# Softmax weights normalised before the transpose instead of attention outputs after the value product

## The reference, cut to what matters

```python
s = einsum(q, k) * scale;  s = where(valid, s, MASK_VALUE)
p = exp(s - max(s));  denom = sum(p);  num = einsum(p, v)
...
den = sum(wts[i] * branches[i][2] for i in range(len(branches)))
return (num / den[..., None]).astype(q.dtype)
```

## Time and profile before

| | us |
|---|---|
| median of 3 runs | 2556.98 (2556.7 to 2559.38) |
| profiled execution, first to last instruction | 2554.3 |
| TensorE busy | 2518.2 (99% of the span) |
| VectorE busy | 1324.1 (52%) |
| ScalarE busy | 567.3 (22%) |
| GpSimd busy | 1519.9 (60%) |

### The profile page before, as it was taken

One profiled execution on the slowest core, in us unless ns is written; L12 is line 12 of the kernel. 1 busy time (PEld: TensorE's weight loads), 2 busy tenths in 40 slices (PEclk: granted clock), 3 DMA queues, 4 the chain that ended last, 5 costly groups with the idle time before them and its releaser, 6 DMA issues.

```text
span 2554.3 us, 33028 instructions
## 1 busy us (share of the span) xinstructions
PE 2518.2 (99%) x11986; PEld 2058.2 (81%) x11986; DVE 1324.1 (52%) x1556; ACT 567.3 (22%) x1033; POOL 1519.9 (60%) x858
## 2 busy tenths in 40 slices
PE   8999999999999999999999999999999988999998
PEld 6888888778888888888888778888887766888887
DVE  6555527656555315556137656555227656655512
ACT  2110014652111001110015552011013564111000
POOL 5666666436666666666665536666664322666664
PEclk9999999999999999999999999999999999999999
DMA  5233222113223223222322113232323111322232
GB/s 169 94 99 99 94 96 75 59 42 98 92 98 99 97 93 99 98 92 98 99 92 74 51 49 99 97 116 98 99 98 134 50 42 34 99 97 93 98 99 74
DMA packets 66724, 228.67 MB, mean 90 GB/s; under 512 B 8784, under 2 KB 11728, under 8 KB 66256
## 3 DMA queue, kind: packets, MB, share of 16 engines
q1 hardware_dynamic: 64928, 225.67, 27.0%
q10 hardware_dynamic: 1712, 1.82, 0.2%
HBM read 225.36 MB, written 2.10 MB: 89 GB/s over the span
## 4 chain that ended last, share of the span: by engine, by line
PE 96%; DVE 2%; ACT 1%; issue 0%; POOL 0%; DMA 0%; SPq 0%; DVEq 0%; POOLq 0%; ACTq 0%
PE bank L610 28%; PE bank L611 28%; PE bank L612 28%; PE bank L627 2%; PE bank L769 2%; PE bank L754 2%; PE bank L738 1%; PE bank L633 1%; PE bank L739 1%; PE bank L992 1%; PE bank L1007 1%; PE bank L984 0%; PE bank L618 0%; PE bank L983 0%; PE bank L899 0%
## 5 line engine op out<-in xcount | busy, mean ns | idle before, releaser
L574 POOL TENSOR_TENSOR wl<-raw,wh 128x1024 fp32r<-128x1024 f32 x412 | 1037.1, 2517 | 34.4
L571 POOL TENSOR_SCALAR wh<-raw 128x1024 fp32r<-128x1024 f32 x412 | 444.8, 1080 | 981.9 <-PE bank L612 944.5
L610 PE MATMUL bank<-xh,wh 128*128 128x512 f32 x2096 | 818.6, 391 | 0.0
L611 PE MATMUL bank<-xl,wh 128*128 128x512 f32 x2096 | 816.4, 389 | 0.0
L612 PE MATMUL bank<-xh,wl 128*128 128x512 f32 x2096 | 816.3, 389 | 0.0
L612 PEld LDWEIGHTS bank<-xh,wl 128*128 128x128 f32 x2096 | 393.5, 188 | 82.7
L610 PEld LDWEIGHTS bank<-xh,wh 128*128 128x128 f32 x2096 | 393.5, 188 | 81.2 <-issue 0.2
L611 PEld LDWEIGHTS bank<-xl,wh 128*128 128x128 f32 x2096 | 393.6, 188 | 81.0 <-issue 0.2
L610 PE MATMUL bank<-acth,wh 128*128 128x512 f32 (+1 forms) x902 | 346.4, 384 | 0.0
L611 PE MATMUL bank<-actl,wh 128*128 128x512 f32 (+1 forms) x902 | 346.2, 384 | 0.0
L612 PE MATMUL bank<-acth,wl 128*128 128x512 f32 (+1 forms) x902 | 346.2, 384 | 0.0
(11 more groups left out here) (273 smaller groups left out, 2352.3 us busy)
## 6 DMA issues: line engine op xcount, KB each, us to landing
raw<-in_stream SPq DMA_DIRECT2D x412, 512.0 KB, 3.6
x<-in_x SPq DMA_DIRECT2D x8, 256.0 KB, 5.9
w1k<-in_w1k SPq DMA_DIRECT2D x1, 2048.0 KB, 9.0
w1v_low<-in_w1v SPq DMA_DIRECT2D x1, 1024.0 KB, 6.7
w1v_high<-in_w1v SPq DMA_DIRECT2D x1, 1024.0 KB, 8.9
out_dram<-x SPq DMA_DIRECT2D x4, 256.0 KB, 2.6
out_dram<-x SPq DMA_DIRECT2D x1, 768.0 KB, 3.7
invcount<-in_c_invcount ACTq DMA_DIRECT2D x1, 512.0 KB, 5.9
```

Source lines behind the costliest of these rows:

```text
L571: nc.gpsimd.tensor_scalar(wh[:, h, :, :], src, 1.0, 1.0, ALU.mult, ALU.mult)\
L574: nc.gpsimd.tensor_tensor(wl[:, h, :, :], src, wh[:, h, :, :].bitcast(F32), ALU.subtract).then_inc(split_done, 1)
L610: mm = nc.tensor.matmul(bank, wh[:, slot, k, :], rh, start=start, stop=False)
L611: mm = nc.tensor.matmul(bank, wh[:, slot, k, :], rl, start=False, stop=False)
```

## The change

Each step's weights are divided by their sum before the turn. VectorE gets `scale_weights(g)`: a reciprocal of one column of `sden`, a wait for it, and a `tensor_scalar` that multiplies the 128 x 512 weights in `sc` in place. It stands right behind the mask instruction of step g + 1. TensorE's `turn(g)` waits for it (`p_done`) and no longer for the exponential. The spread of the reciprocals, their transposes, the copy of the numerators and the product with the rows are gone, with their buffers `on` and `recb`. `high_output` and `low_output` read bank 7 itself, in steps 3 and 4 of the next pair; `values` of a pair waits until `low_output` of the pair before has read the bank. Waits on counts of `ml_done` and `mh_done` are renumbered to the new order.

```diff
@@ TensorE
                 def turn(g):
-                    pe.wait_ge(exp_done, l * STEPS + (g + 1))
+                    pe.wait_ge(p_done, l * STEPS + (g + 1))
...
-                def reciprocal_rows(j):
-
-                    pe.wait_ge(rb_done, l * PAIRS + (j + 1))
-                    pe.wait_ge(vtok_done, l * PAIRS + min(j + 2, PAIRS))
-                    for i in range(NQ):
-                        tr = nc.tensor.transpose(B[6][:, i * P:(i + 1) * P],
-                                                 recb[:, 2 * i:2 * i + 2, :].rearrange("p h d -> p (h d)"), ident[:, :])
-                    tr.then_inc(ot_done, 1)
@@ values
-                        pe.wait_ge(num_done, l * PAIRS + (j + 1))
+                        if l or j:
+                            pe.wait_ge(out_read, l * PAIRS + j)
@@ ScalarE
-                def spread_reciprocals(j):
-                    act.wait_ge(rec_done, l * PAIRS + (j + 1))
-                    nc.scalar.activation(recb[:, :, :], srec[:, :].rearrange("p (c a) -> p c a", a=1)
-                                         .to_broadcast([P, 8, HD]), ACT.Copy).then_inc(rb_done, 1)
-
-                def numerators(j):
+                def high_output(j):
                     act.wait_ge(pv_done, l * HALVES + (2 * j + 4))
-                    nc.scalar.activation(on[:, :], B[7][:, :], ACT.Copy).then_inc(num_done, 1)
-
-                def high_output(j):
-                    act.wait_ge(on_done, l * PAIRS + (j + 3))
-                    nc.scalar.activation(mh1[:, 2 + j, :], on[:, :], ACT.Copy).then_inc(mh_done, 1)
+                    nc.scalar.activation(mh1[:, 2 + j, :], B[7][:, :], ACT.Copy).then_inc(mh_done, 1)
@@ VectorE
-                def reciprocals(j):
-                    dve.wait_ge(exp_done, l * STEPS + (8 * j + 8))
-                    V.reciprocal(srec[:, :], sden[:, j % 2, :]).then_inc(rec_done, 1)
-
-                def normalise(j):
-                    dve.wait_ge(num_done, l * PAIRS + (j + 2))
-                    dve.wait_ge(ot_done, l * PAIRS + (j + 1))
-                    V.tensor_tensor(on[:, :], on[:, :], B[6][:, :], ALU.mult).then_inc(on_done, 1)
+                def scale_weights(g):
+                    e, s = g // 8 % 2, g % 8
+                    dve.wait_ge(exp_done, l * STEPS + (g + 1))
+                    V.reciprocal(srec[:, s:s + 1], sden[:, e, s:s + 1]).then_inc(rec_done, 1)
+                    dve.wait_ge(rec_done, l * STEPS + (g + 1))
+                    V.tensor_scalar(sc[:, g % 3, :], sc[:, g % 3, :], srec[:, s:s + 1], None, ALU.mult).then_inc(p_done, 1)
 
                 def low_output(j, done):
                     dve.wait_ge(mh_done, l * 8 + done)
-                    V.tensor_tensor(ml1[:, 2 + j, :], on[:, :], mh1[:, 2 + j, :].bitcast(F32), ALU.subtract)\
-                        .then_inc(ml_done, 1)
+                    V.tensor_tensor(ml1[:, 2 + j, :], B[7][:, :], mh1[:, 2 + j, :].bitcast(F32), ALU.subtract)\
+                        .then_inc(out_read, 1)
+                    dve.wait_ge(out_read, l * PAIRS + (j + 1))
+                    dve.nop().then_inc(ml_done, 1)
@@ VectorE's loop, step s of pair j
                         V.tensor_tensor_reduce(sc[:, g % 3, :], B[(5, 2)[g % 2]][:, :], band[:, off:off + T], 1.0,
                                                3.0e38, ALU.add, ALU.min, smin[:, s:s + 1]).then_inc(t_done, 1)
+                        if g:
+                            scale_weights(g - 1)
...
-                        if s == 1 and j > 0:
-                            reciprocals(j - 1)
                         if s == 4 and j > 0:
-                            normalise(j - 1)
+                            low_output(j - 1, j if more else 6)
...
-                        if s == 7 and j > 0:
-                            low_output(j - 1, j if more else 7)
```

More of the change, by code:

```diff
@@ L208, in build @@
         pt = sb("pt", [P, 4, T], at=mix1)
-        recb = sb("recb", [P, 8, HD], at=mix1)
         ropet = sb("ropet", [P, 2, T], at=mix1)
@@ L383, in build @@
         rec_done = sem("rec_done")
-        rb_done = sem("rb_done")
-        num_done = sem("num_done")
-        on_done = sem("on_done")
+        p_done = sem("p_done")
+        out_read = sem("out_read")
         zeroed = sem("zeroed")
-        ot_done = sem("ot_done")
         tr_done = sem("tr_done")
@@ L744, in value_turn @@
                     pe.wait_ge(v_evac, l * PAIRS + (j + 1))
-                    pe.wait_ge(on_done, l * PAIRS + (j + 1))
+                    if l or j:
+                        pe.wait_ge(vtok_done, l * PAIRS + j)
                     for kt in range(NQ):
@@ L797, in out_blocks @@
                             if m == 1:
-                                pe.wait_ge(ml_done, l * 8 + 7)
-                        pe.wait_ge(ml_done, l * 8 + (k if 1 < k < 6 else {0: 6, 1: 7, 6: 8, 7: 9}[k]))
+                                pe.wait_ge(ml_done, l * 8 + 8)
+                        pe.wait_ge(ml_done, l * 8 + (k if 1 < k < 6 else {0: 6, 6: 7, 1: 8, 7: 9}[k]))
                         mm = split_product(B[m][:, :], m % 2, k, mh1[:, k, :], ml1[:, k, :], start, stop)
@@ L822, in mixer1 @@
                             values(2 * j - 1)
-                        if s == 3 and j > 0:
-                            reciprocal_rows(j - 1)
                         if s == 6:
@@ L1280, in mixer1 @@
                         if s == 3 and j > 0:
-                            numerators(j - 1)
+                            high_output(j - 1)
                         if s == 4 and more:
                             high_q(l * PAIRS + (j + 1), 1 - e)
-                        if s == (5 if more else 6) and j > 0:
-                            high_output(j - 1)
                         if s == 6 and more:
@@ L1294, in mixer1 @@
                 copy_turn(STEPS - 1)
-                spread_reciprocals(PAIRS - 1)
-                numerators(PAIRS - 1)
                 high_output(PAIRS - 1)
@@ L1735, in pool_low @@
                 def pool_low(t):
[L1736 removed]
+                    dve.wait_ge(mh_done, l * 8 + (5, 7)[t])
                     V.scalar_tensor_tensor(ml1[:, t, :], B[1][:, :], poolscale[:, l, t:t + 1],
                                            mh1[:, t, :].bitcast(F32), ALU.mult, ALU.subtract).then_inc(ml_done, 1)
[L1740 to L1747 removed]
+                def scale_weights(g):
[4 more added lines that the diff above has]
+                    V.tensor_scalar(sc[:, g % 3, :], sc[:, g % 3, :], srec[:, s:s + 1], None, ALU.mult).then_inc(p_done, 1)
                 def low_output(j, done):
                     dve.wait_ge(mh_done, l * 8 + done)
[L1751 to L1752 removed]
+                    V.tensor_tensor(ml1[:, 2 + j, :], B[7][:, :], mh1[:, 2 + j, :].bitcast(F32), ALU.subtract)\
+                        .then_inc(out_read, 1)
+                    dve.wait_ge(out_read, l * PAIRS + (j + 1))
+                    dve.nop().then_inc(ml_done, 1)
                 for j in range(PAIRS):
@@ L1785, in mixer1 @@
                             pool_low(s // 6)
-                        if s == 7 and j > 0:
-                            low_output(j - 1, j if more else 7)
-                reciprocals(PAIRS - 1)
-                normalise(PAIRS - 1)
+                scale_weights(STEPS - 1)
                 low_output(PAIRS - 1, 8)
```

5 lines of the change are left out of this document (removed).

## The result

The kernel after takes 2614.05 us (median of 4 runs, 2610.87 to 2615.26), the kernel before beside it 2556.84: a ratio of 1.0218, 95% interval 1.0206 to 1.023. It is slower, as forecast, by 57 us instead of 39, and outside the range. The profiled execution took 2610.87 us with a span of 2608.7, 54.4 more than the span before; its mean clock was 0.994, that of the other three runs 0.992 to 0.994.

What follows compares the result with a forecast made beforehand. TensorE was taken as the bound, 96% of the chain that ended last. Per layer 22.15 us of new waits less 2.6 saved gave 19.5, 39 over two layers, added to 2557: 2596 us, range 2567 to 2612.

Steps and rivals of the forecast that it cites:

- What bounds the kernel: Whole kernel: TensorE is 96% of the chain that ended last; VectorE has room on average, but in steps with four fill blocks.
- the saving: TensorE: six groups of four transposes of `recb` per layer go, 0.44 us each, 5.3 us over two layers.
- The scaling's price: VectorE: reciprocal 0.15, own wait 0.02, multiplication 0.49, together 0.66 us; on meeting GpSimd it ends 0.28 behind GpSimd's instruction.
- The waits per pair: TensorE in pairs with fill: 2.0 us at step 4's turn, 0.85 at step 6's, 0.3 ahead of scores; 3.15 in all.
- the pooling: End of pairs 0 to 2: GpSimd's pooling step can hold the last low part of k; 1.5 us for the three.
- the sum: Loops of pairs: 22.15 us of new waits less 2.6 saved per layer, 39 us slower over two layers.
- The clock falls: Loops of pairs: waits of 2 us bring TensorE to half clock for a quarter of both loops, 80 us more; chance 0.02.
- VectorE finds the time: Loops of pairs: scalings fall into VectorE's idle stretches only, so the saving alone stays, 2551.7 us; chance 0.05.
- it changes nothing: Whole kernel: saving and waits cancel, 2557 us; chance 0.03.
- No meeting: VectorE's scalings do not wait for GpSimd; step 4's turn waits 0.75 us, total 2567 to 2568 us; chance 0.10.
- Half of it: Loops of pairs: GpSimd's instructions move with TensorE, some scalings miss them; some 25 us more, 2580 us; chance 0.10.

Runs made afterwards that it cites:

- The run with the reciprocals alone: Kernel after the change without the scalings' multiplication; the reciprocal and the turn's wait on it stay: 2555.62 us, ratio 0.9995.
- the run without the wait: Kernel after the change with scalings written to a spare buffer and the turn waiting only for the exponential: 2624.05 us, ratio 1.0265.

## Why the prediction was wrong, and what of it was right

**What bounds the kernel, and the saving**: right. TensorE's chain, idle time of VectorE in the wrong places, and 5.3 us of transposes gone. The run with the reciprocals alone gains only 1.2 of these (3.8 at most by its interval): some 1.7 us of waits stay in its two loops, and eight stops at 0.22 are 1.8 more.

**The scaling's price**: right. 0.16 and 0.49 us plain, and 0.28 behind GpSimd's instruction when it meets one. By the Trainium skill (VectorE: DVE Perf Modes, "The TRN2 errata") I had estimated 0.33 for the 0.49; the trace does not agree, the median of the 96 is 0.487.

**The waits per pair**: right in sum, and part by part only for pairs 1 to 3 and 5. Forecast were 3.15 for every pair with fill and 0.5 more for the pooling in pairs 0 to 2; measured in layer 0 are 3.5, 3.73 and 2.76 in pairs 1 to 3. Pair 4 had 1.70, and 2.65 at its end, where I had 3.15 and 2.3. Pair 5 had 2.6, as forecast. Pair 0 had 5.24, and 0.28 at its end, instead of 3.65; 4.63 of it is a wait that my working did not follow, the fill's on `rope`. That these errors cancel, to 0.1 us in layer 0 and 0.3 in layer 1, is luck.

**The step that failed** is the sum: "Per layer 15.75 + 1.5 + 2.3 + 2.6 = 22.15 us of new waits, less 2.6 saved". It prices a wait at its idle time and lets TensorE go on at its old pace. Two terms were missing, each taken as nothing. Some 41 stops (21 in the loop of layer 0, 20 in that of layer 1, six of them under 0.1 us) at 0.22 are 9.0 us. Stretches at half clock of 3.41, 3.41 and 6.83 us are 13.65 us; 2.28 of these lie in a stop, and in the other 11.4 a matmul begins 0.43 us after the one before it where it was 0.23, so some 5.3 us are lost. With both the sum is 22.2 + 21.9 - 5.3 + 9.0 + 5.3 = 53.1 us, and the spans differ by 54.4; the 1.3 us between them stay open. The median lies 3 us higher than the profiled execution. Its other runs show a mean clock of 0.992 in two of three, so more time at half clock is likely, but they have no trace and it is not shown.

**The rivals.** *The clock falls* had the chance 0.02 because block 2's mixer, busy for 8.52 of 10 us, kept 1.00, and because I thought of a share of the whole loop. It fell in three short stretches, behind stops. The trace of the kernel before had shown such a stretch in the same mixer, 12 us behind that row: a stop of 3.13 us, and 1.4 us behind it 10.24 us at half clock, the only such stretch ahead of the kernel's end.

```profile
2092.00:2100.00 8.00, 4.85 (x36) 3.52 (x31) 7.66 (x16) 5.53 (x13) 0.06 (x1) 0.87 0.21 69
...
2096.51 0.47 PE L983 MATMUL bank<-kh,qs 128*128 128x512 f32 x1 [3.13 <-DVE qs L1908]
```

So the row chosen spoke for the wrong side: a few microseconds further on the clock had fallen behind a stop.

*VectorE finds the time* is refuted by the result and by the run without the wait, *it changes nothing* by the result. *No meeting* is refuted by the 33 long scalings. Its price was put to the test by taking the splits away, and it held: without the bank's wait (2.2 us) the new waits of a loop are 6.9 us, so 2 x 6.9 - 5.3 = 8.5 us where 10.4 were forecast. The 21.4 us measured hold besides the bank's wait, the price of the stops and a stretch of 3.41 us at half clock in each layer. *Half of it* did not come up: meetings are as regular as GpSimd's place in the pair.

## What to carry to other kernels

Price a wait of the bounding engine at its idle time plus what each stop costs by itself, and look for what a long stop does to the clock; here few long stops were dearer than many short ones of about the same sum (29.1 us in 5 stops cost 12.1 more, 26.2 in 19 stops 4.1). When an engine is late, follow everything that hangs on it, the bank releases too: here taking away the wait where it showed moved it on, and only taking work from the late engine helped. A row that speaks against a rival is worth little until its neighbours have been read. Before moving work off the bound, run the version that gives the moved work away for nothing: here it said that there was nothing to win.

## What the runs showed of the hardware

- A stop of TensorE cost 0.22 us beyond its idle time (19 stops at a clock of 1.00, 157.56 us of work instead of 153.46).
- Ten stops of 5.41 to 7.49 us each brought 3.41, 6.83 or 10.24 us at half clock, which began within the stop. The two of 4.6 us after the change brought 3.41 and 6.83 us. Of two stops of 3.5 us one was followed by 3.41 us, and so was a stop of 2.19 us.
- At half clock a matmul of 128 x 512 began 0.43 us after the one before it, at full clock 0.23.
- A `tensor_scalar` of 128 x 512 in SBUF took 0.487 us (median of 96); the 33 that took more than 0.6 us each ended 0.28 or 0.29 behind an instruction of GpSimd.
